# A conditioned mixer of two layers with an expert search behind it: another order in the opening, and conditioning dots on other panels

## The reference

```python
for l in range(DEPTH):
    shift, scale, gate = jnp.split(sc @ w_ada[l] + b_ada[l], 3, axis=-1)          # latent
    shift_c, scale_c, gate_c = jnp.split(sc_ctx @ w_ada[l] + b_ada[l], 3, axis=-1)  # context
    h_lat = rms_norm(x, norm_g[l]) * (1.0 + scale[:, None]) + shift[:, None]
    h_ctx = rms_norm(xc, norm_g[l]) * (1.0 + scale_c) + shift_c
    lat_a, lat_b = mixer_inputs(h_lat, w_in[l], ...)       # p = h @ w_in, then q, k, v, gates
    ctx_a, ctx_b = mixer_inputs(h_ctx, w_in[l], ...)
    ...                                                    # two attentions
    x = x + gate[:, None] * merge_groups(o_a, lat_a[3], o_b, lat_b[3], w_out[l])
    if l < DEPTH - 1:
        xc = xc + gate_c * merge_groups(...)
```

## Time and profile before

| | |
|---|---|
| median of 3 runs | 3299.45 us (3289.32 to 3300.81) |
| profiled execution | 3295.02 us, its span 3293.2 us |
| TensorE busy | 2973.2 us, 90% |
| VectorE busy | 2420.8 us, 74% |
| ScalarE / GpSimd busy | 1178.8 us / 689.9 us |
| conditioning dots on VectorE (L2045) | 208, 486.2 us |
| granted TensorE clock, mean | 0.955 |

### The profile page before, as it was taken

The page is one execution under the profiler, slowest core; times in us unless marked ns, Lnnn a source line. Parts: engine busy times, 40 slices in busy tenths (PEclk is TensorE's granted clock), DMA queues, the critical chain, the costliest instruction groups (busy, mean ns, idle before and its releaser), DMA issues.

```text
span 3293.2 us, 39034 instructions
## 1 busy us (share of the span) xinstructions
PE 2973.2 (90%) x14844; PEld 2303.9 (70%) x14844; DVE 2420.8 (74%) x3398; ACT 1178.8 (36%) x1810; POOL 689.9 (21%) x732
## 2 busy tenths in 40 slices
PE   7999999999889999998999999999999996766666
PEld 3678887467667998588999899788888884322223
DVE  2378986756877876468664564898988996988886
ACT  3332324133124444155544554444444442111111
POOL 0000000001320000014000000222221214777773
PEclk8999999999999999999999999999999998888888
DMA  9654672435775786548444443999999999999996
GB/s 399 238 192 178 257 280 91 166 141 205 297 288 218 288 326 232 214 165 324 155 160 146 169 151 145 363 405 419 407 413 405 418 397 372 390 409 409 409 410 278
DMA packets 160666, 932.73 MB, mean 283 GB/s; under 512 B 21600, under 2 KB 42336, under 8 KB 53216
## 3 DMA queue, kind: packets, MB, share of 16 engines
q0 software_dynamic: 75264, 503.46, 38.8%
q1 hardware_dynamic: 71392, 403.70, 31.5%
q10 hardware_dynamic: 13824, 23.07, 1.9%
HBM read 900.80 MB, written 29.36 MB: 282 GB/s over the span
## 4 chain that ended last, share of the span: by engine, by line
PE 63%; DVE 15%; DMA 9%; POOL 5%; issue 4%; ACT 2%; DVEq 0%; SPq 0%; PEld 0%; PEldq 0%; ACTq 0%; POOLq 0%
PE psum L1197 28%; PE psum L1142 17%; PE psum L1206 5%; DMA memh<-dots,memr 4%; DVE w_lo L1531 3%; DVE psum L2554 3%; PE psum L1398 3%; DMA memr<-in_ada_dram 3%; PE psum L1417 2%; DVE junk L2045 2%; POOL memh L998 2%; POOL memr L1010 2%; DMA memh<-in_panels_dram 1%; PE psum L1166 1%; POOL sq L962 1%
## 5 line engine op out<-in xcount | busy, mean ns | idle before, releaser
L1531 DVE TENSOR_TENSOR w_lo<-memr,w_hi 128x1024 fp32r<-128x1024 f32 x614 | 741.9, 1232 | 326.3 <-ACT w_hi L1524 325.7
L1524 ACT ACTIVATE w_hi<-memr 128x1024 fp32r<-128x1024 f32 x614 | 642.0, 1057 | 830.5 <-PE psum L1197 384.0
L1197 PE MATMUL psum<-h_hi,w_hi 128*128 128x512 f32 (+1 forms) x1600 | 568.1, 355 | 28.4 <-DVE w_lo L1531 27.9
L1197 PE MATMUL psum<-h_lo,w_hi 128*128 128x512 f32 (+1 forms) x1600 | 553.3, 346 | 0.0
L1197 PE MATMUL psum<-h_hi,w_lo 128*128 128x512 f32 (+1 forms) x1600 | 552.8, 346 | 0.0
L2045 DVE CUSTOM_DVE_ANT_0 junk<-memr 128x2048 bf16<-128x2048 f32 x208 | 486.2, 2338 | 58.4 <-DMA memr<-in_ada_dram 56.6
L1142 PE MATMUL psum<-w_hi,l_hi 128*128 128x512 f32 x1024 | 399.8, 390 | 5.4 <-DVE w_lo L1531 4.7
L1439 PE MATMUL psum<-memr,memh 128*128 128x512 f32 x456 | 250.2, 707 | 165.8 <-ACT memh L1987 147.9
L1142 PE MATMUL psum<-w_lo,l_hi 128*128 128x512 f32 x1024 | 398.9, 390 | 0.0
L1142 PE MATMUL psum<-w_hi,l_lo 128*128 128x512 f32 x1024 | 398.9, 390 | 0.0
L1197 PEld LDWEIGHTS psum<-h_hi,w_hi 128*128 128x128 f32 x1600 | 306.6, 192 | 75.8 <-DVE w_lo L1531 30.6
(11 more groups left out here) (296 smaller groups left out, 4517.9 us busy)
## 6 DMA issues: line engine op xcount, KB each, us to landing
memr<-in_panels_dram SPq DMA_DIRECT2D x343, 1024.0 KB, 7.3
memr<-in_ada_dram POOLq DMA_DIRECT2D x160, 1024.0 KB, 5.1
dots<-sq ACTq DMA_DIRECT2D x64, 256.0 KB, 9.9
memh<-in_panels_dram SPq DMA_DIRECT2D x12, 1024.0 KB, 9.7
memr<-in_xin_dram SPq DMA_DIRECT2D x4, 1024.0 KB, 7.7
gstore<-sq ACTq DMA_DIRECT2D x16, 256.0 KB, 4.2
memh<-gstore SPq DMA_DIRECT2D x2, 2048.0 KB, 8.0
memr<-gstore SPq DMA_DIRECT2D x2, 2048.0 KB, 9.7
```

What stands on the lines that cost most here:

```text
L1197: ins = pe.matmul(bank(o["bank"])[:, 0:o["w"]], w_[:, c, :], x_[:, kc, :], start=kc == 0 and j == 0, stop=kc == DC - 1 and j == 2)
L1524: act.activation(hi, a, ACT.Copy).then_inc(hi_ready, 1)
L1531: dve.tensor_tensor(lo_, a, hi.bitcast(F32), ALU.subtract).then_inc(lo_ready, 1)
```

## The change

Three things are changed.

1. In `pe_opening` the products of block 0 (12 matmuls for each of four panels) are done for three panels ahead of `rows(8)`, for the fourth behind it, and then rows 9 to 15 and the columns of block 1 follow; before, one feature chunk of all four panels stood between each two rows. Blocks 1 to 3 keep their order.
2. `begin` no longer makes TensorE, ACT and DVE wait for each other at the head of the first in-projection.
3. The table of chunks: the first in-projection gets 46 chunks for 42 (two vectors each), the up-projection behind it 16 for 14, the out-projection of the first layer 32 for 40, and the second layer's up-projection 12 for 10. Its panels of cq/ckv then read 1, 1, 1, 2, 1, 2, 2, 2 (before 1, 1, 1, 2, 1, 2, 1, 2), its panels of g 1, 2, 2, 1, 2, 2, 1, 2, 2, 1, 2, 2, 1, 2, 0, 0 (before 1, 2, 2, 1, 2, 1, 2, 2, 1, 2, 1, 2, 1, 2, 0, 0). The up-projection reads 3, 2, 3, 3, 2, 3, 0 (before 2, 3, 2, 2, 3, 2, 0), with chunks 46 and up, of which only 46 and 47 have two vectors (before chunks 42 to 47 have two). The out-projection reads 2, 3, 2, 2, 2, 3, 2, 2, 3, 2, 2, 2, 3, 2, 0, 0 (before 3, 3, 3, 2, 3, 3, 3, 3, 3, 3, 2, 3, 3, 3, 0, 0).

```diff
-        spread(COND, 42, [0] * 5 + [1.0] * 12 + [1.4] * 18 + [0] * 2)
+        spread(COND, 46, [0] * 5 + [1.1] * 12 + [1.4] * 18 + [0] * 2)
...
-        spread(COND + 44, 40, [1] * 14 + [0] * 2)
+        spread(COND + 44, 32, [1] * 14 + [0] * 2)
...
-            if me != "sp" and "follows" in st or me == "pe" and "after_split" in st:
+            if me != "sp" and ("follows" in st or "quad" in st) or me == "pe" and "after_split" in st:
                 upto = 0
...
-            for b in range(BLOCKS - 1):
-                for j in range(4):
-                    rows(8 * (b + 1) + 2 * j)
-                    rows(8 * (b + 1) + 2 * j + 1)
-                    if j == 2:
-                        columns(b + 1, 0)
-                    if b == 1:
-                        products(quad[j], range(4, 8))
-                        if j == 3:
-                            columns(b + 1, 1)
-                        continue
-                    for i, o in enumerate(quad):
-                        if j == 3 and i == 2:
-                            columns(b + 1, 1)
-                        products(o, [4 * b + j])
+            for o in quad[0:3]:
+                products(o, range(4))
+            rows(8)
+            products(quad[3], range(4))
+            for n in range(9, 16):
+                rows(n)
+                if n == 13:
+                    columns(1, 0)
+            columns(1, 1)
+            for j, o in enumerate(quad):
+                rows(16 + 2 * j)
+                rows(17 + 2 * j)
+                if j == 2:
+                    columns(2, 0)
+                products(o, range(4, 8))
+            columns(2, 1)
+            for j in range(4):
+                rows(24 + 2 * j)
+                rows(25 + 2 * j)
+                if j == 2:
+                    columns(3, 0)
+                for i, o in enumerate(quad):
+                    if j == 3 and i == 2:
+                        columns(3, 1)
+                    products(o, [8 + j])
```

More of the change, by code:

```diff
@@ L423, in spread @@
                 ada_after[first + j] = round(chunks * at / sum(weights)) - round(chunks * before / sum(weights))
-        spread(COND, 42, [0] * 5 + [1.0] * 12 + [1.4] * 18 + [0] * 2)
-        spread(COND + 37, 14, [1] * 6 + [0])
-        spread(COND + 44, 40, [1] * 14 + [0] * 2)
+        spread(COND, 46, [0] * 5 + [1.1] * 12 + [1.4] * 18 + [0] * 2)
+        spread(COND + 37, 16, [1] * 6 + [0])
+        spread(COND + 44, 32, [1] * 14 + [0] * 2)
         for j, n in enumerate([1, 1, 2, 2, 2] + [1, 1, 0, 1, 1, 1, 1, 1] + [1] * 4 + [2] * 4 + [1] * 15 + [0]):
             ada_after[COND + 60 + j] = n
-        spread(COND + 97, 10, [1] * 6 + [0])
+        spread(COND + 97, 12, [1] * 6 + [0])
         spread(COND + 104, N_ADA - 2 * DC - 148, [1] * 13 + [0] * 3)
```

## The result

| | before | after |
|---|---|---|
| runs beside each other, median | 3296.1 us (4 runs, 3289.3 to 3300.8) | 3257.9 us (4 runs, 3257.5 to 3258.6) |
| profiled execution | 3295.02 us, span 3293.2 | 3258.64 us, span 3256.8 |

The ratio is 0.9886, with a 95% interval of 0.9866 to 0.9906: faster, by 38 us, where 3254 us were forecast (3244 to 3275).

A forecast was written before the change was run, and what follows sets the result against it. Main bound addressed: TensorE's stops for VectorE's late weight-panel halves in the first layer's out-projection. Terms -33.9 - 3.0 - 4.3 - 0.3 + 0.9 - 2.0 = -42.6 us took 3295.0 to 3252.4, forecast as 3254 us (3244 to 3275).

The forecast's parts named there:

- Out-projection: First layer's out-projection: TensorE's stops for VectorE's late low halves go, except 1.2 us at panel 1; 33.9 us gained.
- Behind it: After the out-projection: last residual and column sum no longer wait for VectorE's late split; 3.0 us gained, between 0 and 3.3.
- Up-projections: First layer's stop before the rotation goes, 2.0 us gained (0 to 2); second layer's two extra dots cost nothing.
- In-projection: First in-projection, 46 chunks for 42: one stop at the cq/ckv panels, 0.9 us lost, between 0 and 6.
- Barrier: Head of the first in-projection: 2.65 us idle and 1.7 us of lower clock go; 4.3 us gained, at least 0.
- The opening's order: Opening: block 1's shift columns come at 72.3 to 73.8; 0.3 us gained, between 1.1 gained and 3 lost.
- wrong in a step: Signs in the later profile that a step failed; for the opening, block 1's shift columns later than 74 us.
- a rival with another price: Opening: the 3 us empty queue comes through in full and the next two blocks are as late: 9 us, 3263; chance 0.06.
- The sum: Whole kernel: the six terms add to -42.6 us, from 3295.0 to 3252.4 us.

The follow-up runs named there:

- The two experiments on the table: Against new table, no barrier, old opening order (3253 us): out-projection's four three-dot panels in a row, 3257.0 us; at most two dots a panel there, 3253.7 us.
- no barrier alone: The kernel before without the barrier at the head of the first in-projection, nothing else changed: 3293.5 us, ratio 0.9999.
- the table alone: The kernel before with only the new table of chunks, opening's order and barrier as they were: 3253.3 us, and 3256.6 us when repeated.
- the last experiment: Changed kernel with rows 8 to 12 early (3252.0 us), plus panel 12's second chunk moved to 11 and out-projection threes on panels 2, 5, 8, 11: 3252.7 us.

## Why the prediction was right, and the step that failed

**Out-projection: right, 33.9 against 33.5 us.** One stop of 1.2 us at panel 1's second half, as worked out, and every other panel 10.88 us apart. The two experiments on the table show why: a single three is hidden by the slack, four in a row are not, and dropping the last four dots gains 1.5 us. In the seven traces with this table for the out-projection that stop was 1.2 to 1.5 us in six and 3.2 in one, so the size holds in most executions, not in all. That the agreement is to 0.4 us is luck in part.

**Behind it: right, 3.0 against 3.1.** The load of the last panels came in time, and the residual sum no longer waited for VectorE.

**Up-projections: right, 2.0 against 2.3,** the stop at the rotation. The lower clock didn't follow that stop in the profiled execution; where it did (no barrier alone, 101.5 us) the same stop was worth 4.0. The second layer's up-projection took 77.6 us before and after, the 0 that was forecast; with four dots more than that it took 5.2 us more, so the 0 holds for the two dots of this change, not for six.

**In-projection: right in size, 0.9 against 0.9, wrong in place.** The 0.9 measured is from the opening's last product to the stage's, the changed kernel against no barrier alone. The prediction put the stop at cq/ckv, with VectorE 8 us late; there was none, and the forecast's own 8 us against half as much room would give a stop of some 4 us, not 0.9. What there was, 0.7 us, stood at kr. The new table changes the panels ahead of cq too, which the list of changes leaves out: panels 5 to 12 get 1, 2, 1, 1, 2, 1, 1, 2 chunks (before 1, 1, 1, 2, 1, 1, 1, 1), and the last of them is kr. VectorE waited 2.4 us for TensorE just before kr, so could not start early, and a rotation waited behind the dots. The agreement in size is luck.

**Barrier: 4.3 against 3.8 at the head; less at the end.** The mechanism is as described, and no other wait took its place there. The term counted the idle time and the dip as sure. The dip is not: two of the five traces with a barrier don't have it, and there the price is 2.4. At the end of the runs the three pairs of kernels that differ in the barrier give 1.0 us (give or take 1.9), 1.9 (3.6) and 4.1 (2.8), weighted 2.0 (1.4). That the dips behind later stops move when the program shifts is seen in one place (the up-projection's stop of 2.0 us, without a dip before and with one without the barrier). Whether that accounts for the rest is argued, not shown.

**The opening's order: the step that failed.** It said 0.3 us gained, the shift columns of block 1 at 72.3 to 73.8. They came at 75.9, past the mark set for "wrong in a step", and with the dip the opening ended 4.2 us late in this pair of traces, 5.5 by the mean of all traces. Two numbers of the step were off. It took row 8's buffer for the only late one, and the queue for busy until 60.3 us; it ran out at about 57.7, and load 14 had to wait as well, for row 9, which stands behind the fourth panel's products at 63.3. So 5.1 us of the queue were lost, not up to 3, and TensorE, with all 48 products spent, had nothing left for the last wait: 2.9 us idle, then half clock. The prediction had this as a rival with another price (9 us, chance 0.06); the runs give 4.9 to 5.7 (three pairs of kernels by their means), and in this pair of traces the loss was made by block 2's shift columns (100.4 against 96.2 us); the last block added nothing (124.1 against 119.8). The place is uncertain by some 2 us for another reason: with the order of before the same columns stood between 70.7 and 73.7 us in the traces.

**The sum.** From -42.6: 4.5 from the opening, 0.5 from the barrier, and 1.5 lost behind the seam between the layers give -36.1, against 36.4 between the spans; the other terms' small differences cancel. At the seam (the first product of the second layer) the changed kernel was 37.9 us ahead, at the end of its span 36.4. That part isn't settled. The stretch from the seam to the end varied by several us without any difference in the program, as with the table alone (2309.8 and 2305.2 us). It took 2306.6 to 2307.2 us in the three traces with the old table, and 2305.0 to 2310.8, in the mean 2308.6, in the nine that have the new one behind the seam (two dots more). So a loss of 1 to 2 us there may be real; no run looks for its place.

## What to carry to other kernels

Side work on an engine that is nearly in balance should be judged by the worst run of panels, not by the stage's mean: work out how far ahead of need a result is ready, how much one heavy panel overdraws and a light one gives back, and place them accordingly. Before moving an instruction in an order written by hand, list the buffers that its use frees and the transfers that wait for them; pull uses that free a buffer forward, and hold back work that frees nothing as filler for the waits (done together here, not one by one). A gain of a few microseconds at one place may not be there at the end: compare the end of many runs, and the place in the trace, and say which of the two is shown.

## What the runs showed of the hardware

A stop of TensorE has no fixed price. The same 2.65 us at the same place were followed by half clock (1.2 GHz) in three traces and not in two: 3.8 or 2.4 us.

VectorE's dot beside GpSimd's addition of squares takes 3.01 us (the 828.38 row) or 3.1 instead of 2.29, and GpSimd's addition 2.6 us where it took 1.29 with no dot beside it. Near the end of the out-projection of before, then in the last experiment (GpSimd, then VectorE):

```profile
971.59 1.29 POOL L962 TENSOR_TENSOR sq<-sq 128x512 f32<-128x512 f32 x1 [2.98 <-ACT sq L1582]
```

```profile
809.04 2.59 POOL L965 TENSOR_TENSOR sq<-sq 128x512 f32<-128x512 f32 x1 [2.98 <-ACT sq L1597]
```

```profile
808.20 2.28 DVE L2060 CUSTOM_DVE_ANT_0 junk<-memr 128x2048 bf16<-128x2048 f32 x1
...
810.66 3.12 DVE L2060 CUSTOM_DVE_ANT_0 junk<-memr 128x2048 bf16<-128x2048 f32 x1
```

One dot ends at 810.5, the next begins at 810.66. The addition, 1.29 us by itself, ended at 811.6, and the second dot is as late as if it had begun there. The dot has both its inputs, the rows and the conditioning vector, in SBUF. By the Trainium skill (SBUF — State Buffer, Who interferes with whom, and its Summary) a VectorE operation with two inputs in SBUF and a GpSimd operation that reads SBUF exclude each other, and the second waits until the first ends; the trace agrees. Since POOL issues the third dot's load behind that addition, that load is asked for 1.3 us later as well.
